# Two feed-forward layers: the up-units of chunks two to four as Strassen blocks, squared on ScalarE

## The reference

```python
D_FF = 4 * D_MODEL          # 4096

def sq_relu_mlp(h, w1, w2):
    a = jax.nn.relu(h @ w1)
    return (a * a) @ w2

    for i in range(DEPTH):  # 2
        ...
        x = x + y
        h = rms_norm(x, norm_ffn[i])
        x = x + sq_relu_mlp(h, ffn_w1[i], ffn_w2[i])
```

## Time and profile before

| | |
|---|---|
| median of 3 runs | 2352.24 us (2351.30 to 2353.12) |
| profiled execution | 2353.43 us, its span 2351.2 us |
| TensorE matmuls | 2303.0 us busy, 98% |
| VectorE | 1616.3 us, 69% |
| ScalarE | 1164.0 us, 50% |
| GpSimd | 62.7 us, 3% |
| one feed-forward chunk | 82.9 us, twice four of them |
| DMA | 278 MB, 118 GB/s over the span |

### The profile page before, as it was taken

How to read it: one execution, slowest core, us unless ns; L and a number is a source line. 1 busy time by engine, 2 the same in 40 slices (tenths; PEclk the granted TensorE clock), 3 DMA queues, 4 the chain that set the end, 5 groups by cost and what they waited for, 6 DMA issues and landing times.

```text
span 2351.2 us, 34723 instructions
## 1 busy us (share of the span) xinstructions
PE 2303.0 (98%) x12638; PEld 1996.3 (85%) x12638; DVE 1616.3 (69%) x2473; ACT 1164.0 (50%) x1910; POOL 62.7 (3%) x76
## 2 busy tenths in 40 slices
PE   7999999999999999999999999999999999999999
PEld 5788888888888887888888888989976777898997
DVE  7877777767566576867566568857756986883773
ACT  5655555544233246864233236625646566662563
POOL 0000000000000000000000000101100000010110
PEclk9999999999999999999999999999999999999999
DMA  4222222235455442014455444746722113374671
GB/s 157 81 75 78 80 80 77 75 93 179 132 161 179 153 134 71 19 42 167 133 161 178 151 144 113 194 120 156 200 77 64 65 47 90 85 197 118 155 196 54
DMA packets 97189, 278.17 MB, mean 118 GB/s; under 512 B 12704, under 2 KB 13216, under 8 KB 96672
## 3 DMA queue, kind: packets, MB, share of 16 engines
q1 hardware_dynamic: 84464, 256.72, 33.7%
q0 software_dynamic: 10368, 18.88, 5.3%
q10 hardware_dynamic: 2224, 0.79, 0.2%
HBM read 274.25 MB, written 2.10 MB: 118 GB/s over the span
## 4 chain that ended last, share of the span: by engine, by line
PE 62%; issue 28%; DMA 5%; DVE 3%; ACT 1%; POOL 0%; POOLq 0%; SPq 0%; DVEq 0%; ACTq 0%
PE psum L607 17%; PE psum L608 17%; PE psum L609 17%; DMA raw<-twin 4%; PE psum L671 1%; PE psum L1120 1%; PE psum L854 1%; PE psum L855 1%; PE psum L853 1%; PE psum L702 1%; PE psum L731 1%; PE psum L724 1%; DVE w_lo L2056 0%; POOL raw L591 0%; PE psum L707 0%
## 5 line engine op out<-in xcount | busy, mean ns | idle before, releaser
L607 PE MATMUL psum<-h_hi,w_hi 128*128 128x512 f32 x1192 | 464.6, 390 | 7.5 <-DVE w_lo L2056 2.7
L1304 ACT ACTIVATE w_hi<-raw 128x1024 fp32r<-128x1024 f32 x297 | 310.8, 1052 | 305.5 <-PE psum L609 295.4
L2056 DVE TENSOR_TENSOR w_lo<-raw,w_hi 128x1024 fp32r<-128x1024 f32 x313 | 381.5, 1220 | 108.3 <-ACT w_hi L1304 106.7
L608 PE MATMUL psum<-h_lo,w_hi 128*128 128x512 f32 x1192 | 453.1, 380 | 0.0
L609 PE MATMUL psum<-h_hi,w_lo 128*128 128x512 f32 x1192 | 452.9, 380 | 0.0
L607 PEld LDWEIGHTS psum<-h_hi,w_hi 128*128 128x128 f32 x1192 | 226.1, 190 | 46.8 <-issue 9.3
L608 PEld LDWEIGHTS psum<-h_lo,w_hi 128*128 128x128 f32 x1192 | 226.4, 190 | 31.8 <-issue 2.6
L609 PEld LDWEIGHTS psum<-h_hi,w_lo 128*128 128x128 f32 x1192 | 226.2, 190 | 31.7
L1460 ACT ACTIVATE w_hi<-raw 128x512 fp32r<-128x512 f32 x252 | 150.4, 624 | 93.5 <-DVE raw L2540 41.2
L609 PE MATMUL psum<-f_hi,w_lo 128*128 128x512 f32 x512 | 194.3, 379 | 0.0
L608 PE MATMUL psum<-f_lo,w_hi 128*128 128x512 f32 x512 | 194.3, 379 | 0.0
(11 more groups left out here) (374 smaller groups left out, 4783.9 us busy)
## 6 DMA issues: line engine op xcount, KB each, us to landing
raw<-stream SPq DMA_DIRECT2D x313, 512.0 KB, 3.6
raw<-twin SPq DMA_DIRECT2D x180, 256.0 KB, 4.2
ada_raw<-ada_in SPq DMA_DIRECT2D x72, 512.0 KB, 4.0
raw<-twin POOLq DMA_DIRECT2D x72, 256.0 KB, 4.3
x<-x_in SPq DMA_DIRECT2D x2, 1024.0 KB, 6.6
out<-x SPq DMA_DIRECT2D x8, 256.0 KB, 2.4
a_mask<-mask_in SPq DMA_DIRECT2D x1, 1024.0 KB, 9.6
crow<-crow_in SPq DMA_DIRECT2D x2, 512.0 KB, 5.7
```

The source lines that it names most:

```text
L607: nc.tensor.matmul(o, whi, xh, start=start, stop=False)
L608: nc.tensor.matmul(o, whi, xl, start=False, stop=False)
L1304: A(w_hi[:, slot(u0), :], raw[:, slot(u0), :], ACT.Copy).then_inc(S["hi"], 1)
L2056: V.tensor_tensor(w_lo[:, sl, :], raw[:, sl, :], f32(w_hi[:, sl, :]), ALU.subtract).then_inc(S["lo"], 1)
```

## The change

In each layer chunk one stays as it is, with the sums of the inputs added to its steps (`ffn_operands`: h is rebuilt from its parts, summed as `operands` does, split). In chunks two to four the 8 up-units become four pairs, 28 blocks, run by `ffn_chunk` on every engine, and the hardware loops are unrolled. What follows a pair is different from SwiGLU: ScalarE takes relu (in SBUF, of the upper result with scale -1) and then Square of it, each waiting for the one before, and converts it; the lower result's relu has two halves, one in SBUF and one from PSUM. VectorE keeps only the low parts of the results. The last block s4 lies inside the first down-unit. The conditioning products of these chunks move from the up-units to the down-units, and three of their tiles are loaded among the block copies. The first blocks of the next chunk are copied, added and split during the down-units. The half-slot helpers (`g` in place of `c`) count ten groups of pairs instead of four. Small operations of the recurrent rates (`rates`) move between down-units; `b_cos` and `b_sin` lie elsewhere in SBUF.

The core of the diff:

```diff
+SW = 2 * (FFN_CHUNKS - 1)
+PAIRS = [4] * SW + [HALF - n for n in STD]
...
+                for i in range(1, FFN_CHUNKS):
+                    g = 3 * layer + i - 1
+                    c = 4 * layer + i
+                    u0 = unit_after(g)
+                    load_blocks(g, 0 if i == 1 else 4, 9)
+                    load_ada(c * ADA_TILES, 0)
+                    load_blocks(g, 9, 14)
+                    load_ada(c * ADA_TILES + 1, 1)
+                    load_blocks(g, 14, 19)
+                    load_ada(c * ADA_TILES + 2, 2)
+                    load_blocks(g, 19, BLOCKS[g])
+                    for n in range(4):
+                        load_after_blocks(g, n)
+                    for n in range(4, 8):
+                        load_unit(u0 + n, slot(u0 + n), back=4)
+                        load_ada(c * ADA_TILES + n - 1, (n - 1) % 3)
+                    if i < FFN_CHUNKS - 1:
+                        load_blocks(g + 1, 0, 2)
+                    else:
+                        load_unit(u0 + 8, slot(u0 + 8), back=4)
+                    load_ada(c * ADA_TILES + 7, 1)
+                    if i < FFN_CHUNKS - 1:
+                        load_blocks(g + 1, 2, 4)
+                    else:
+                        load_unit(u0 + 9, slot(u0 + 9), back=4)
+                    load_ada(c * ADA_TILES + 8, 2)
 
...
+            def ffn_chunk(layer, i):
+                g = 3 * layer + i - 1
+                c = 4 * layer + i
+                u0 = unit_after(g)
+                n = BLOCKS[g]
+                def left(q, which):
+                    if q == 0:
+                        return after("F_x", 8 * c - 4 + which)
+                    if q == 1:
+                        return after("F_x", 8 * c - 1)
+                    return (after("F_s", 8 * c + 2 * q - 3), combined(g, q - 2, 1), combined(g, q - 2, 0))[which]
+                for b in range(n - 1):
+                    strassen_block(g, b, FFN_IN[layer], FFN_SUMS[layer], left, layer if i == 1 else None)
+                pe.wait_ge(*after("lo", u0))
+                pe.wait_ge(*after("F_s", 8 * c + 5))
+                for k in range(KT):
+                    if k == 2:
+                        strassen_block(g, n - 1, FFN_IN[layer], FFN_SUMS[layer], left)
+                    pe.wait_ge(*after("F_lo", 8 * c + k))
+                    m = mm3(bank(0), tile_of(w_hi, slot(u0), k), tile_of(w_lo, slot(u0), k), f_hi[:, k, :], f_lo[:, k, :],
+                            k == 0, k == KT - 1)
+                m.then_inc(S["mm"], 1)
+                for d in range(1, KT):
+                    if d == 3:
+                        pe.wait_ge(*after("F_x", 8 * c - 1))
+                    elif d > 3:
+                        pe.wait_ge(*after("F_x", 8 * c + d - 4))
+                    unit(u0 + d, slot(u0 + d), bank((0, 1, 2, 6)[d % 4]), f_hi, f_lo)
 
             def bank_left(c, q, i):
 
...
+            def squared_upper(g, c, q):
+                t = f_g[:, q % 2, 1, :]
+                act.wait_ge(*combined(g, q, 2))
+                A(t, t, ACT.Relu, scale=-1.0).then_inc(S["F_r"], 1)
+                act.wait_ge(*relu_event(c, 2 * q))
+                A(t, t, ACT.Square).then_inc(S["F_s"], 1)
+            def squared_lower(g, c, q, b):
+                t = f_g[:, q % 2, 0, :]
+                act.wait_ge(*combined(g, q, 0))
+                A(halves(t)[:, 0], halves(t)[:, 0], ACT.Relu)
+                act.wait_ge(*block_done(g, b))
+                A(halves(t)[:, 1], by_parity(bank(3 * (q % 2), 256)), ACT.Relu).then_inc(S["F_r"], 1)
+                act.wait_ge(*relu_event(c, 2 * q + 1))
+                A(t, t, ACT.Square).then_inc(S["F_s"], 1)
+            def ffn_chunk(layer, i):
+                g = 3 * layer + i - 1
+                c = 4 * layer + i
+                u0 = unit_after(g)
+                n = BLOCKS[g]
+                last = i == FFN_CHUNKS - 1
+                for b in range(n + 1):
+                    kind, q = PLANS[g][b - 1] if b else (None, None)
+                    if kind == "a11":
+                        snap(g, b - 1, 0)
+                        if q == 1:
+                            act.wait_ge(*after("mm", u0 - 1))
+                        if q:
+                            squared_upper(g, c, q - 1)
+                            f_high(c, 2 * q - 2)
+                    if kind == "s3":
+                        snap(g, b - 1, 1)
+                    if kind == "s2":
+                        snap(g, b - 1, 2)
+                        if q:
+                            f_high(c, 2 * q - 1)
+                    if b == n:
+                        squared_upper(g, c, q)
+                        f_high(c, KT - 2)
+                    if kind == "s4":
+                        squared_lower(g, c, q, b - 1)
+                    if b == n:
+                        f_high(c, KT - 1)
+                    for s in HI_ORDER[g]:
+                        if hi_step(g, s) == b:
+                            block_split(g, s)
+                    if b in (n - 4, n - 2, n - 1, n):
+                        split_after_blocks(g, (n - 4, n - 2, n - 1, n).index(b))
...
+                def f_low(k):
+                    dve.wait_ge(*after("F_hi", 8 * c + k))
+                    V.tensor_tensor(f_lo[:, k, :], f_g[:, (k // 2) % 2, 1 - k % 2, :], f32(f_hi[:, k, :]), ALU.subtract).then_inc(S["F_lo"], 1)
+                for b in range(n + 1):
+                    kind, q = PLANS[g][b - 1] if b else (None, None)
+                    if kind == "a12":
+                        combine(b - 1, 0)
+                    if kind == "a22":
+                        combine(b - 1, 1)
+                    if kind == "s1":
+                        combine(b - 1, 2)
+                    for s in LO_ORDER[g]:
+                        if lo_step(g, s) == b:
+                            block_low_part(g, s)
+                    for m in range(1, PAIRS[g]):
+                        if AT[g]["s2", m] - 4 == b:
+                            first_weights_sum(g, m)
+                        if AT[g]["s2", m] - 3 == b:
+                            second_weights_sum(g, m)
+                    if kind == "s3" and q:
+                        f_low(2 * q - 2)
+                    if kind == "a12" and q:
+                        f_low(2 * q - 1)
+                    if b in (n - 3, n - 1):
+                        low(u0 + (n - 3, n - 1).index(b), slot(u0 + (n - 3, n - 1).index(b)))
+                f_low(KT - 2)
+                f_low(KT - 1)
+                low(u0 + 2, slot(u0 + 2))
+                low(u0 + 3, slot(u0 + 3))
+                condition_tile(c, 0)
+                for d in range(KT):
+                    if 1 <= d < (7 if last else 5):
+                        low(u0 + d + 3, slot(u0 + d + 3))
+                    if not last and d == 5:
+                        block_low_part(g + 1, 0)
+                        block_low_part(g + 1, 1)
+                    if not last and d == 6:
+                        first_weights_sum(g + 1, 0)
+                        block_low_part(g + 1, 3)
+                        second_weights_sum(g + 1, 0)
+                    condition_tile(c, d + 1)
+                    if layer == 0 and i == 1 and d in (1, 2, 3):
+                        rates(d)
+                    if last and d >= 2:
...
```

More of the change, by code:

```diff
@@ L81 @@
 BLOCKS = [len(p) for p in PLANS]
-BLOCK0 = [sum(BLOCKS[:c]) for c in range(4)]
+BLOCK0 = [sum(BLOCKS[:g]) for g in GROUPS_OF_PAIRS]
 AT = [{p: b for b, p in enumerate(blocks)} for blocks in PLANS]
@@ L2462, in _ @@
             condition(1)
[L2463 to L2466 removed]
+            ffn(1)
             def ada_cols(sub, kind):
```

776 lines of the change are left out of this document (423 added, 353 removed).

## The result

| | before | after |
|---|---|---|
| median of five runs, us | 2352.24 | **2363.36** |
| ratio to before, 95% interval | | 1.0038, 1.0022 to 1.0053 |
| profiled execution, its span, us | 2353.43, 2351.2 | 2363.36, 2361.6 |

The change makes the kernel 0.4% slower; 2336.5 was forecast, 0.7% faster.

What follows compares the result with a forecast made beforehand. TensorE, busy 2303 of 2351 us, was taken as the bound. A chunk gains 3.92 us minus a 1.3 us stall, 2.6; six chunks gain 15.7, so 2336.5 us from 2352.24. Range 2328.5 to 2348.0 us.

Steps and rivals of the forecast that it cites:

- Pitches: In chunks two to four: 5.18 us a unit, 1.340 a block; gain 3.92 us a chunk, 23.5 over six.
- The ring: Per up-phase pair, ScalarE and VectorE waiting in turn need 9.96 us against TensorE's 9.38; stall 1.3 us a chunk.
- the walk: Times from a chunk's first block: last s1's low part due 34.64, ends 34.98; down-units begin 1.3 us late.
- The DMA way: Third pair's s3: added copy arrives at 14.9, ScalarE at 15.6; tile in front taken as nothing, bound about 1.8 us.
- Rival C: DMA decides in the up phases: tile delays the added copy, stall 3.3 us a chunk, 2348.5 us; chance 0.14.
- Chunk one's sums: Input sums in each layer's first chunk, 16 us on VectorE, 4.2 on ScalarE, hidden in VectorE's 33 us free.
- No wait in the first chunk: Sign to look for in the trace: TensorE has no wait in the first chunk, where the input sums lie.
- Rival D: Slower: handoffs of 0.12 us instead of 0.03 make the pair ring 11.1 us; 5.0 a chunk, 2358.7; chance 0.08.
- Rival A: Ring of ScalarE and VectorE never bites in the up phases, no TensorE wait: 2328.7 us; chance 0.21.
- The range: Whole kernel: from rival A, 2328.5 us, to most of rival C, 2348.0 us.

Runs made afterwards that it cites:

- the fastest kernel: Kernel after with tiles two and three between down-unit loads, chunk one's splits a unit later, upper half squared on VectorE at its step's end: 2335.0 us, 0.9915 of before.

## Why the prediction was wrong, point by point

**Pitches: right.** 78.96 us without a stall was summed (77.62 from chunk one to two); the three chunks of the fastest kernel in which hardly anything was waited for took 79.06, 79.06 and 77.83 us, so the 1.340 us of a block and the 5.18 us of a unit hold. The gain of 3.92 us a chunk is real. The rule of the Trainium skill, page TensorE: Matmul & The Clock Gate, section Back-to-back issue gap, with 131 ns at 512 columns, would have had the change lose 2 us a chunk with nothing waiting. No run here agrees with it: distances down to 79.06 in place of 82.88 show that the narrower matmuls are cheaper here. That its time, some 2364 us, lies beside the measured 2363.4 is chance: in the fastest kernel the pitches in the new chunks are 216 and 112 ns, as the prediction had them, and the loss is waits.

**The ring: right in mechanism and size.** 9.96 us a pair summed, 9.95 measured. A stall of 1.3 us a chunk forecast, 1.24 to 1.43 measured with the tiles out of the way and 1.30 to 1.36 in after once ScalarE's DMA wait is taken out. The place was right too: with the tiles out of the way 0.9 us at the first down-unit's low part, and 0.3 in front of s1, where the walk had 34.98 against 34.64.

**The DMA way: the step that failed.** The failed term is the wait for the added block s3 of the third pair, put at nothing. The prediction had the added copy arrive at 14.9 and ScalarE at 15.6 us after the chunk's first block, called that "just fits", and bounded the tile in front by 1.8 us, of which it took nothing. ScalarE came at 15.7 in the chunk of the first fence, as summed, and got the block at 19.6. The term is 1.7 to 4.5 us a chunk, mean 3.5, in place of 0. Two choices made it. The bound counted one tile, by the time it adds in front of a copy; the second tile and the addition on GpSimd's queue weren't counted, and the addition alone went from 4.6 us to 6.5 to 8.6. And the way of 10.4 us was taken from SwiGLU, where no tiles are loaded, so that "just fits" had no margin: with both tiles out of the way the block came at 15.7, with ScalarE free at 15.6. That lateness passes to the chain in full was in the prediction (14.9 + 1.8 is 1.1 behind 15.6, "of which 1.1 would pass to the chain") and was right; its bound was too small. Rival C was this mechanism, at 3.3 us a chunk in all; it was 4.8 (29.0 / 6), and 0.75 more for chunk one (4.5 / 6). The mean DMA share of 0.8 that C also counted on was not reached: it is 0.69 in the up phase, and 0.67 in one without a wait.

**Chunk one's sums: hidden as work, not as order.** 33 us of free VectorE time were there, but the prediction asked only for the load. The split of the first sum was queued on ScalarE one unit too early, in front of a unit's weights. 4.5 us in all. "No wait in the first chunk" was the sentence that after refutes.

**Rival D** (slower through longer handoffs) had the sign and not the cause. Handoffs are 0.03 to 0.04 us (with the tiles moved, a relu at 645.36 of 0.63 us and its square at 646.03). **Rival A** was reached by none, but the fastest kernel, where the ring is shorter, has the three chunks named above within about 0.2 us of it.

**The range** ended at C. By its own argument a row with a share of 0.75 and a ScalarE that waits for this DMA today should have carried more than 0.14, and its bound should have included both tiles.

## What to carry to other kernels

When a change leaves two queues in a ring whose turn is longer than the main engine's, a delay on the ring's own path is paid in full (six chunks of six here), so each transfer that the ring waits for needs a margin of its own, read under the traffic of that very stage and not of a calmer one. Before large loads with no hurry are left among small urgent ones, ask where in the order they can stand: here moving two 512 KB tiles turned 0.4% slower into 0.4% faster; with the squaring on VectorE, chunk one's splits moved and the tiles between the down-unit loads it is 0.85%. After shortening a ring, look for what comes last now: here it was the next addition. Ask of moved work not only whether the engine has the time but what stands behind it in the queue while it waits.

## What the runs showed of the hardware

- An accumulating 256 KB addition on GpSimd's queue lands after 4.6 us in the median of after, but after 6.5 to 8.6 us in the six places where 512 KB tiles and 256 KB copies are in flight on SyncE's queue (in one of them these take 7.4 and 5.3), and after 4.9 to 6.5 with the tiles moved. With only 8 columns of the two tiles loaded the kernel is 17 us faster.
- A wait of TensorE of 2.0 to 3.0 us was followed in some cases by 3.4 us near half the granted clock (0.50 to 0.54 over the stretch), in others not (2.48 us with the upper half squared on VectorE; 2.12, 1.76 and 1.49 us in after; 9 of 12 waits of 2.0 us). It cost 1.7 to 1.8 us where TensorE set the pace and nothing measurable where the ring did.
- With matmuls of this kind in a stream, 256 columns take 112 ns and 512 take 216 ns from start to start, at full granted clock (the fastest kernel, in chunks two to four).
